# Asking for gamma and beta before the last expert pair ends, a second PSUM bank for its last half, and four more weight places while experts run

## What is computed

```python
def layer_norm(x, g, b):
    x32 = x.astype(F32)
    mu = jnp.mean(x32, axis=-1, keepdims=True)
    var = jnp.mean(jnp.square(x32 - mu), axis=-1, keepdims=True)
    return ((x32 - mu) * lax.rsqrt(var + LN_EPS) * g.astype(F32) + b.astype(F32)).astype(x.dtype)
...
    # grouped_moe: two experts of one group of four are chosen for each token
    h = jax.nn.silu(jnp.einsum('td,edf->etf', xt, w1)) * jnp.einsum('td,edf->etf', xt, w3)
    h = h * gates.T[:, :, None].astype(h.dtype)
    y = jnp.einsum('etf,efd->td', h, w2)
```

## Time and profile before

| | us |
|---|---|
| times of three runs | 1398.04, 1399.77, 1395.88 |
| their median | 1398.04 |
| the profiled execution's own time | 1400.55 |
| its span | 1398.7 |
| TensorE busy | 1293.8 (93% of the span) |
| VectorE busy | 615.4 (44%) |
| ScalarE busy | 470.3 (34%) |
| DMA: bytes over the span | 338.33 MB |

### The profile page before, as it was taken

The page is one execution under the profiler, slowest core; times in us unless marked ns, Lnnn a source line. Parts: engine busy times, 40 slices in busy tenths (PEclk is TensorE's granted clock), DMA queues, the critical chain, the costliest instruction groups (busy, mean ns, idle before and its releaser), DMA issues.

```text
span 1398.7 us, 18499 instructions
## 1 busy us (share of the span) xinstructions
PE 1293.8 (93%) x7912; PEld 938.7 (67%) x7912; DVE 615.4 (44%) x808; ACT 470.3 (34%) x636; POOL 205.6 (15%) x207
## 2 busy tenths in 40 slices
PE   7999999988999999998999999968886899999994
PEld 6999988865799999887754444326885665444431
DVE  6644466753676664396511111126455551111113
ACT  5544436553446444244311111114565331101011
POOL 0000000500499980030000000000123000000000
PEclk9999999996999999899999999988998999999998
DMA  9555553520555554426679999993421568999994
GB/s 374 182 185 186 191 190 124 201 98 1 175 188 188 181 181 159 151 69 228 251 282 419 421 421 422 421 409 109 138 73 52 181 240 311 419 421 420 421 420 171
DMA packets 47750, 338.33 MB, mean 242 GB/s; under 512 B 5296, under 2 KB 5296, under 8 KB 7728
## 3 DMA queue, kind: packets, MB, share of 16 engines
q1 hardware_dynamic: 45936, 330.53, 61.6%
q10 hardware_dynamic: 1728, 6.55, 1.3%
HBM read 336.02 MB, written 1.05 MB: 241 GB/s over the span
## 4 chain that ended last, share of the span: by engine, by line
PE 82%; DVE 9%; DMA 5%; ACT 3%; issue 1%; SPq 0%; POOL 0%; ACTq 0%; DVEq 0%
PE pb L177 81%; DMA ring<-in_moe_w 3%; DVE halves L295 2%; DMA XN<-in_ln_b 1%; ACT halves L287 1%; DMA ring<-in_ffn_w 1%; DVE SM L1437 1%; DVE Xs L1448 1%; PE pb L1874 0%; DVE Xs L387 0%; DVE p L1603 0%; DVE Xs L389 0%; DVE XN L326 0%; DVE p L1617 0%; DVE Xs L1443 0%
## 5 line engine op out<-in xcount | busy, mean ns | idle before, releaser
L295 DVE TENSOR_TENSOR halves<-ring,halves 128x2048 fp32r<-128x2048 f32 (+1 forms) x122 | 285.4, 2354 | 159.7 <-ACT halves L287 159.5
L177 PE MATMUL pb<-XTh,halves 128*128 128x256 f32 x1856 | 340.1, 284 | 13.5 <-DVE p L1617 7.5
L177 PEld LDWEIGHTS pb<-XTh,halves 128*128 128x128 f32 x1856 | 292.3, 192 | 15.8 <-DVE p L1617 8.1
L177 PE MATMUL pb<-XTl,halves 128*128 128x256 f32 x928 | 263.0, 283 | 0.0
L287 ACT CAST halves<-ring 128x2048 fp32r<-128x2048 f32 (+1 forms) x122 | 227.3, 1873 | 104.5 <-PE pb L177 100.6
L177 PE MATMUL pb<-ring,gather 128*64 128x512 f32 x1024 | 233.4, 598 | 3.8 <-DVE gather L2003 1.7
L177 PEld LDWEIGHTS pb<-XTl,halves 128*128 128x128 f32 x928 | 178.5, 192 | 0.9
L177 PE MATMUL pb<-halves,XTh 128*128 128x512 f32 x512 | 160.8, 395 | 6.6 <-DVE halves L295 3.1
L177 PEld LDWEIGHTS pb<-ring,gather 128*64 128x64 f32 x1024 | 71.4, 137 | 134.7 <-issue 130.5
L177 PE MATMUL pb<-ring,slots_ht 128*64 128x512 f32 x512 | 118.5, 605 | 3.6 <-DMA ring<-in_moe_w 2.6
L177 PEld LDWEIGHTS pb<-halves,XTh 128*128 128x128 f32 x512 | 96.2, 190 | 27.9 <-DVE halves L295 3.9
(11 more groups left out here) (343 smaller groups left out, 1297.9 us busy)
## 6 DMA issues: line engine op xcount, KB each, us to landing
ring<-in_moe_w SPq DMA_DIRECT2D x192, 1024.0 KB, 13.6
ring<-in_ffn_w SPq DMA_DIRECT2D x66, 1024.0 KB, 4.9
ring<-in_w_tok SPq DMA_DIRECT2D x10, 1024.0 KB, 4.9
ring<-in_ple_gate SPq DMA_DIRECT2D x8, 1024.0 KB, 4.9
ring<-in_w_out SPq DMA_DIRECT2D x4, 1024.0 KB, 4.9
ring<-in_ab_out SPq DMA_DIRECT2D x4, 1024.0 KB, 4.9
ring<-in_sb_v SPq DMA_DIRECT2D x4, 1024.0 KB, 23.9
ring<-in_sb_q SPq DMA_DIRECT2D x4, 1024.0 KB, 10.9
```

Of the source, the lines that this page charges most:

```text
L177: return e.matmul(out, l, r, start=start, stop=stop, **kw)
L295: e.tensor_tensor(l, raw_of(n), h.bitcast(F32), ALU.subtract).then_inc(*low.mark(n))
```

## The change

Five edits. (1) While experts run, four places more: two where XTh and XTl lie, which are last read by the matmuls of the gate (`ple_gate`), and two where `gate_sig` and `ple` lie, free after `ple_added`. An expert block then waits for the block 16 ahead of it. (2) `down(7, 1)` writes bank 5 instead of bank 4 and waits only for `mul(7, 0)`. (3) `spread(7, 0)` stands behind `down(7, 1)`. (4) ScalarE asks for gamma and beta within the experts, behind `high(6, 1)`, having waited for the last `gather`. (5) Behind layer 0, TensorE transposes t = 0 between its two stretches of `idle`, and the second stretch no longer waits for the variance and writes bank 0. The branch for an expert with more than 64 tokens (`dense`) is fitted to the new places; it doesn't run here.

```diff
+EXTRA = 4
...
         for n in range(len(plan)):
-            at = min(range(RING + SPLIT if n in whole else RING), key=lambda s: latest[s])
+            if n in whole and n - 1 not in whole:
+                latest[RING + SPLIT:] = [n - 1] * EXTRA
+                fresh = {RING + SPLIT + 2, RING + SPLIT + 3}
+            at = min(range(RING + SPLIT + EXTRA if n in whole else RING), key=lambda s: latest[s])
+            if n in whole and at in fresh:
+                fresh.remove(at)
+                after_ple[n] = max(i for i in range(2) if index[("moe", i), "w13", 0, 0, 0] <= n)
...
+        extra = [place(f"extra{i}", at, SCOLS) for i, at in enumerate((xt_at, xt_at + 2048, rest, rest + 4096))]
...
                 if gone[n] >= 0:
                     e.wait_ge(*used.at(gone[n]))
+                if n in after_ple:
+                    e.wait_ge(*ple_added.at(after_ple[n], 2))
                 e.dma_start(raw_of(n), src).then_inc(land[home[n]], 16)
...
-        def pe_turn(e, key, src3, ready):
+        def pe_turn(e, key, src3, ready, between=None):
             for t in range(2):
+                if t and between:
+                    between()
                 e.wait_ge(*ready(t))
...
+        def down_bank(p, h):
+            return banks[5 if p == 7 and h else 4]
...
             def down(p, h):
-                D = banks[4]
-                if h:
+                D = down_bank(p, h)
+                if h and p < 7:
                     e.wait_ge(*s.y_low.at(p, 0))
+                elif h:
+                    e.wait_ge(*s.mul.at(7, 0))
...
-                    if n == 1 and p >= 1:
+                    if n == 1 and 1 <= p < 8:
                         spread(p - 1, 0)
...
                     if p >= 1:
                         down(p - 1, n)
+            spread(7, 0)
             spread(7, 1)
...
                     if p >= 1:
                         high(p - 1, n)
+                if p == 7:
+                    e.wait_ge(*s.gathered.at(7, 1))
+                    act_norm_load(e, 2 * i + 1)
...
                 if i:
                     e.wait_ge(*x_new.at(("moe", 0), 0))
                     idle(3)
-                    e.wait_ge(*variance.at(1, 1))
-                    idle(2)
-                    pe_turn(e, "stick", X3, normed_x(1))
+                    pe_turn(e, "stick", X3, normed_x(1), lambda: idle(2, banks[0]))
                     pe_stick(e)
...
-                e.wait_ge(moe_half[i], 1)
-                act_norm_load(e, 2 * i + 1)
                 act_norm(e, 2 * i + 1)
```

More of the change, by code:

```diff
@@ L244, in build @@
             whole.update(range(first, len(plan)))
-        home, high_home, gone, high_gone, landed = [], [], [], [], []
-        latest, landings = [-1] * (RING + SPLIT), [0] * (RING + SPLIT)
+        home, high_home, gone, high_gone, landed, after_ple = [], [], [], [], [], {}
+        latest, landings = [-1] * (RING + SPLIT + EXTRA), [0] * (RING + SPLIT + EXTRA)
         for n in range(len(plan)):
-            at = min(range(RING + SPLIT if n in whole else RING), key=lambda s: latest[s])
+            if n in whole and n - 1 not in whole:
[5 more added lines that the diff above has]
+                after_ple[n] = max(i for i in range(2) if index[("moe", i), "w13", 0, 0, 0] <= n)
             home.append(at)
@@ L261, in build @@
                 latest[at] = n
-        land = [sem(f"land{i}") for i in range(RING + SPLIT)]
+        land = [sem(f"land{i}") for i in range(RING + SPLIT + EXTRA)]
         high, low, used = signal("w_high"), signal("w_low"), signal("w_used")
+        extra = [place(f"extra{i}", at, SCOLS) for i, at in enumerate((xt_at, xt_at + 2048, rest, rest + 4096))]
         def place_of(x, s, n):
+            if s >= RING + SPLIT:
+                return extra[s - RING - SPLIT][:, 0:plan[n].shape[-1]]
             return x[:, s * SCOLS:s * SCOLS + plan[n].shape[-1]]
@@ L2029, in dve_slots @@
                         low(p - 1, n)
-        GG, gT = place("dense_gates", rest, 4096), place("dense_gate_t", rest + 4096, 256)
-        HTD = [[place(f"dense_ht{p}{x}", rest + 4608 + 2048 * p + 1024 * x, 1024).rearrange("p (c t) -> p c t", c=4)
+        GG, gT = place("dense_gates", rest + 10496, 4096), place("dense_gate_t", rest + 14848, 256)
+        HTD = [[place(f"dense_ht{p}{x}", rest + 6144 + 2048 * p + 1024 * x, 1024).rearrange("p (c t) -> p c t", c=4)
                 for x in range(2)] for p in range(2)]
-        SD = [place(f"dense_silu{x}", rest + 8704 + 512 * x, 512) for x in range(2)]
-        XD = place("dense_x", xt_at, 2048)
+        SD = [place(f"dense_silu{x}", rest + 15104 + 512 * x, 512) for x in range(2)]
+        XD = place("dense_x", rest + 2048, 2048)
         XD3 = XD.rearrange("p (k t) -> p k t", k=8)
@@ L2077, in pe_dense @@
             e.wait_ge(*ple_added.at(i, 2))
+            for kp in range(4):
+                for k in range(2):
+                    for t in range(2):
+                        j = e.transpose(banks[kp][:, k * 256 + t * 128:k * 256 + t * 128 + 128],
+                                        XN3[:, t, (2 * kp + k) * 128:(2 * kp + k + 1) * 128], ident)
+            j.then_inc(*f.x_turned.mark())
             for t in range(2):
@@ L2120, in dve_dense @@
             e.tensor_copy(gT[0:16, :], banks[4][0:16, 0:256]).then_inc(*f.kept.mark())
-            e.tensor_tensor(XD, XTh.bitcast(F32), XTl.bitcast(F32), ALU.add).then_inc(*f.whole.mark())
+            e.wait_ge(*f.x_turned.at())
+            for kp in range(4):
+                j = e.tensor_copy(XD[:, kp * 512:kp * 512 + 512], banks[kp][:, :])
+            j.then_inc(*f.whole.mark())
             for p in range(8):
@@ L2154, in pe_program, with idle @@
         def pe_program(e, c):
-            def idle(n):
+            def idle(n, P=banks[7]):
                 for _ in range(n):
-                    mm(e, banks[7][:, :], ident, CO[:, 0:512], True, True)
+                    mm(e, P[:, :], ident, CO[:, 0:512], True, True)
             e.wait_ge(l_con, 16)
```

8 lines of the change are left out of this document (5 added, 3 removed).

## The result

The changed kernel's median was 1376.2 us in four executions (1374.38 to 1379.59), beside 1397.03 for the kernel before: a ratio of 0.9846, 95% interval 0.9818 to 0.9874, or 21 us less. The forecast was 1382.4, 15.6 us less, with a range from 1378.5: the way was right, the size too small, and the time 2.3 us outside of the range. The same two kernels, timed twice more, came nearer to each other: 0.9874 (0.9851 to 0.9896) and 0.9861 (0.9826 to 0.9895). Over all executions, 16 of the changed kernel and 78 of the kernel before, the medians are 1378.6 and 1397.0, 18.4 us apart.

A forecast was written before the change was run, and what follows sets the result against it. TensorE held 82% of the span, so the gain was what it waits for: 10.98 us in layer 0 plus 4.60 in layer 1, 15.6 off the 1398.04 median, giving 1382.4 us; range 1378.5 to 1387.

The forecast's parts named there:

- What bounds it, and the places: Experts: four places fill 10.2 us of unused DMA time, removing last-pair weight waits, 1.30 us in layer 0, 1.86 in layer 1.
- My sum: Whole kernel: gains of 10.98 us in layer 0 and 4.60 in layer 1, together 15.6 us.
- The second bank: Last pair: down(7, 1) starts directly behind down(7, 0), 2.72 us less in layer 0, 2.74 in layer 1.
- Gamma and beta, and XTh: Behind layer 0: beta lands in time, so XTh starts 14.75 us behind the last spread, 6.96 less; layer 1 gains nothing.
- case A: Behind layer 0: beta still late, ScalarE's requests served behind SyncE's blocks; 3 us less gained, 1385.5 us; chance 0.07.
- The rule on branches: Behind layer 0's last spread: TensorE's 5.07 us gap belongs to the branch over unused `dense` and travels with the spread's end.
- case B: Behind layer 0: TensorE ends last, its gap doubled by full DMA queues; at most 5.8 us lost, 1385 to 1388; chance 0.11.
- bounds of what the trace doesn't show: Clock at layer 0's end (1.7 us either way), next stage's start (1.5 us gain), branch gap (0 to 5 us lost).
- case C: Layer 0's last pair and next stage's start: the clock helps, 1.7 + 1.5 = 3.2 us more, 1379.2 us; chance 0.13.

The follow-up runs named there:

- e3: Changed kernel without its four more places (12, as in the kernel before): 1383.86 us, ratio 0.9900 to the kernel before.
- e5: Changed kernel with gamma and beta asked for behind the experts again: 1386.17 us, ratio 0.9923 to the kernel before.
- e11: Kernel before with only the second bank and the moved spread: 1392.48 us, ratio 0.9971.
- e4: Changed kernel with its last half back in bank 4 and the spread back in front of it: 1387.83 us, ratio 0.9916 to the kernel before.
- after: First profile of the changed kernel; its four executions had a median of 1376.2 us, ratio 0.9846 to the kernel before.
- e2: Changed kernel, unchanged, timed and profiled again: 1380.5 us, ratio 0.9874 to the kernel before.
- e13: Changed kernel, unchanged, a third time: 1378.07 us, ratio 0.9861 to the kernel before.
- before: First profile of the kernel before, without the change; the profiled execution took 1400.55 us, the median of the three shown was 1398.04.
- e1: Kernel before, unchanged, timed and profiled again: 1397.01 us in 12 executions, ratio 1.0002.
- e8: Changed kernel with fewer splits ahead of XTh and XTl and no second idle stretch: 1372.9 us, ratio 0.9836 to the kernel before.
- e14: Changed kernel with fewer splits ahead of XTh and XTl and no second idle stretch, run again: 1376.92 us, ratio 0.9852 to the kernel before.
- e9: Kernel before with the four more places alone: 1385.83 us, ratio 0.9917.
- e10: Kernel before with only gamma and beta asked for early, behind high(6, 1): 1390.91 us, ratio 0.9958.
- e12: Changed kernel with fewer splits ahead of XTh and XTl, idle stretch kept: 1377.66 us, ratio 0.9861 to the kernel before.

## Why the prediction was right and where not

**What bounds it, and the places.** Right in mechanism: the idle 10 us were filled, and all waits for weights went. The term, 3.2 us, was too small, for what the places do alone (8.8 us) and for what they add to the other parts (5.0, of which 4.0 are the waits for weights in e3). The waits had been read one at a time, as if each edit worked on the kernel before by itself. My sum gave the whole 6.97 us behind layer 0 to the early load, though some 3 of them come with the places too.

**The second bank.** Right in mechanism, and a little small in size: 2.7 us in each layer forecast, and 2.95 in both layers when it is undone. The missing 0.2 us is that the 32 matmuls of both `down` in a row take 7.09 us, where two stretches of 16 take 2 x 3.65 = 7.30.

**Gamma and beta, and XTh.** Right to the hundredth: 14.75 us forecast, 14.74 or 14.75 measured, in all profiles that have the early load and the four splits. ScalarE's request stood at 907 to 908 us instead of 916, because the experts began sooner; beta was there 5 us ahead of its need (907.75 + 11.4 = 919.2, wanted at 924.4). So case A did not come: from 913 to 918 us ScalarE's queue got 35% of the engines' time beside SyncE's blocks, as in the earlier trace rows. For layer 1 I priced the load at nothing. That holds for the kernel before, but with the second bank it saves 0.7 to 0.8 us there (e5, e11).

**The rule on branches.** The gap behind the last spread was 4.8 to 5.2 us in 15 of the 16 profiles, before and after the change: it travels with E, and case B, a doubled gap, did not come. This agrees with what the Trainium skill (Runtime: NRT & Kernel Launch, Instruction fetch mechanics) says of a taken branch, but no run takes the branch away, so the cause is not shown. And one profile speaks for some part of the queues. In e4 the gap is 3.44 us:

```profile
933.81 5.49 PE L178 MATMUL pb<-CO 128*128 128x512 f32 x6 [3.44 <-issue]
```

There the DMA engines were busy for a share of 0.18 during the gap; in the other 15 profiles it was 0.61 to 1.02. It is one profile, so this stays a hint.

**Where it was wrong: the bounds of the clock, and terms that were too small.** The step that failed is "bounds of what the trace doesn't show". There I kept the clock as it was, put both of its gains at 1.7 and 1.5 us into case C, and let the range end at 1378.5, only 0.7 us beyond that case. Three things were missing.

First, the dip at the last pair was gone with the change, and I had priced that at nothing: in six layer ends of after, e2 and e13 there is none, in four of the kernel before (before, e1) there are three, of 1.7 us. From the table, means of two profiles of before and three of after: S to E 236.3 - 230.0 = 6.3 in layer 0, E to V 23.3 - 16.2 = 7.1, S to E 236.9 - 231.7 = 5.2 in layer 1, together 18.6 us, against the sum's 15.6. Of the surplus of 3.0, the dips are 2.5. The slower start of layer 1's experts takes 0.8 back; that is likely chance, since e5 to e8 and e14, nearly the same kernel, start as before does.

Second, the other 1.3 are terms of the sum that were too small: without the clock's parts the stretch from S to E became shorter by 4.6 us in layer 0 and 5.2 in layer 1, where I had 4.02 and 4.60, and E to V by 7.1, where I had 6.96. A wait's idle time is some 0.2 us less than what it costs, since the matmuls on its two sides also don't follow each other without a break.

Third, in the stages without any edit the granted clock differs from execution to execution, and that is larger than any term of the sum. 78 executions of the kernel before have a median of 1397.0 us and reach from 1390.2 to 1403.8; 16 of the changed one have 1378.6, from 1372.9 to 1383.7. The difference, 18.4 us, is close to the 18.6 of the profiles. The first four executions of the changed kernel, at 1376.2, were luckier by 2.4 us; the three of before that I started from, at 1398.04, less so by 1.0. Time falls by 1.0 us for each 0.001 of mean clock in both kernels.

So the 6.2 us between 1382.4 and 1376.2 come apart as 1.3 of terms too small, 1.7 of clock within the experts, and 3.4 of chance in two small samples, less 0.2 by which the profiles exceed the medians. So about half of the miss is luck: the median of all 16 executions lies 0.1 us within the range. Case C, "the clock helps", named the right cause with the wrong half of it: the 1.7 in the last pair came more often than not, while the next stage started at the upper level in one of three profiles (e2).

**What stays open.** Whether the dip in the last pair is gone because of the change, or by chance. Counting by the order of the last half: with `down(7, 1)` behind the spread, as before (before, e1, e4, e9, e10), 4 of 10 layer ends have it; with its own bank, 2 of 22 (e3 and e14). That leans to the change, but e9 and e10, in the old order, show none. A fit of time on mean clock puts the two kernels at 1395.2 and 1380.5 us at 0.970, 14.7 us apart, near the sum without the clock; but mean clock is itself a result of how long TensorE waits. Why e4's gap behind the experts is shorter stays open too.

## What to carry to other kernels

Look at each end of a stage for the transfers that the next one has asked for already: a small load asked for late stands behind or beside them, and either asking sooner or letting the queue run dry sooner repairs the same wait, so the two gains don't add. Where a path can be read to the hundredth, but the kernel's executions spread by 13 us and the forecast starts from a median of three, the range must hold the spread of a median of few executions, not the bounds of the path alone; read the granted clock of the stages that an edit can't reach before believing in a surplus. And a lead that is used up only at the very end needs only as many places as the end is late: two did as much as four.

## What the runs showed of the hardware that I had not expected

The same instructions of the state-space stage ran at 0.50 or at 1.00 of the clock in different executions of one kernel, with nothing else changed, which moved all that follows by 6.1 us. The experts' first 45 us came in three lengths, 1.6 us apart, with a granted clock of 1.00, 0.93 or 0.86 over 25 us. Between two stretches of matmuls behind layer 0, gaps of 0.8 to 1.9 us were followed by the upper level in four of four profiles (e12, e14, e8, e2); behind gaps of 2.4 to 3.4 us both levels came: upper in e10 (2.4) and e11 (3.1), lower in before (2.4) and after (3.0). TensorE's gap behind the last spread of layer 0 was 3.4 us in the one profile in which the DMA engines' share was down to 0.18 (e4), and 4.8 to 5.2 us in the others, with shares of 0.61 and more.
